# Stick-breaking attention with the queries on the partitions: a reversed scan of sigmoids, turned by TensorE, times differences of the values

## The reference

```python
def stick_breaking_attention(q, k, v):
    # beta[t,s] = sigmoid(q_t.k_s / sqrt(Dh)), s < t
    # A[t,s]    = beta[t,s] * prod_{s<j<t} (1 - beta[t,j])
    ...
        z = jnp.einsum("bqhd,bkhd->bhqk", qb, kb) * scale
        mask = s_idx < t_idx
        log_beta = jax.nn.log_sigmoid(z)
        log_one_minus = jnp.where(mask, jax.nn.log_sigmoid(-z), 0.0)
        tail = lax.cumsum(log_one_minus, axis=3, reverse=True) - log_one_minus
        weights = jnp.where(mask, jnp.exp(log_beta + tail), 0.0)
        outs.append(jnp.einsum("bhqk,bkhd->bqhd", weights, vb))

def second_block(...):
    h = rms_norm(x, norm1_g[layer])
    q, k, v, glu_a, glu_b = jnp.split(h @ w_in[layer], splits, axis=-1)
    q, k = rms_norm(q, q_norm_g), rms_norm(k, k_norm_g)      # per head
    attn = stick_breaking_attention(q, k, v)
    c = glu_a * jax.nn.sigmoid(glu_b)
    c = causal_depthwise_conv(c, conv_dw_w, conv_dw_b)
    c = jax.nn.silu(layer_norm(c, conv_ln_g, conv_ln_b))
    x = x + jnp.concatenate([attn, c], axis=-1) @ w_out
    ...
```

## Time and profile before

| | |
|---|---|
| median of 3 runs | 1230.31 us (1230.0 to 1230.79) |
| the profiled execution | 1230.45 us, its span 1228.7 us |
| TensorE busy | 1222.5 us, 99% of the span |
| weight loads of TensorE | 1004.1 us, beside the matmuls |
| VectorE, ScalarE, GpSimd busy | 593.9, 505.4, 585.3 us |
| granted clock of TensorE | full in all 40 slices |
| chain that ended last | TensorE 93%, VectorE 5%, ScalarE 1% |

### The profile page before, as it was taken

How to read it: one execution, slowest core, us unless ns; L and a number is a source line. 1 busy time by engine, 2 the same in 40 slices (tenths; PEclk the granted TensorE clock), 3 DMA queues, 4 the chain that set the end, 5 groups by cost and what they waited for, 6 DMA issues and landing times.

```text
span 1228.7 us, 16447 instructions
## 1 busy us (share of the span) xinstructions
PE 1222.5 (99%) x5590; PEld 1004.1 (82%) x5590; DVE 593.9 (48%) x870; ACT 505.4 (41%) x677; POOL 585.3 (48%) x473
## 2 busy tenths in 40 slices
PE   9999999999999999999999999999999999999998
PEld 7988888888888888888888886768888888888887
DVE  6782435434653165414675898764333223321431
ACT  7532443343443144323464247675433223332331
POOL 5875553233445344463465652134444434444444
PEclk9999999999999999999999999999999999999999
DMA  7444332122232322232233221102222322223222
GB/s 299 138 138 135 105 103 69 52 69 69 103 102 103 103 85 87 101 120 72 77 125 103 103 86 52 35 18 86 87 102 88 117 86 102 93 83 116 81 77 82
DMA packets 34035, 118.41 MB, mean 96 GB/s; under 512 B 4033, under 2 KB 4161, under 8 KB 33857
## 3 DMA queue, kind: packets, MB, share of 16 engines
q1 hardware_dynamic: 33696, 117.49, 27.9%
q10 hardware_dynamic: 288, 0.24, 0.1%
HBM read 115.61 MB, written 2.10 MB: 96 GB/s over the span
## 4 chain that ended last, share of the span: by engine, by line
PE 93%; DVE 5%; ACT 1%; POOL 0%; issue 0%; POOLq 0%
PE ps L1258 29%; PE ps L1259 29%; PE ps L1260 29%; DVE ps L1126 2%; DVE slab L1126 2%; PE ps L1582 2%; PE ps L1425 1%; PE ps L1563 1%; PE ps L1324 0%; PE ps L1350 0%; PE ps L1623 0%; POOL squares L443 0%; PE ps L1440 0%; PE ps L1399 0%; PE ps L1536 0%
## 5 line engine op out<-in xcount | busy, mean ns | idle before, releaser
L365 POOL TENSOR_TENSOR w_lo<-w_raw,w_hi 128x512 fp32r<-128x512 f32 x430 | 557.3, 1320 | 610.3 <-ACT w_hi L476 355.8
L1258 PE MATMUL ps<-xg_hi,w_hi 128*128 128x512 f32 x960 | 375.8, 391 | 0.0
L1260 PE MATMUL ps<-xg_hi,w_lo 128*128 128x512 f32 x960 | 373.6, 389 | 0.0
L1259 PE MATMUL ps<-xg_lo,w_hi 128*128 128x512 f32 x960 | 373.6, 389 | 0.0
L1258 PE MATMUL ps<-y_hi,w_hi 128*128 128x512 f32 (+1 forms) x608 | 230.9, 380 | 0.0
L1259 PE MATMUL ps<-y_lo,w_hi 128*128 128x512 f32 (+1 forms) x608 | 229.8, 378 | 0.0
L1260 PE MATMUL ps<-y_hi,w_lo 128*128 128x512 f32 (+1 forms) x608 | 229.8, 378 | 0.0
L1260 PEld LDWEIGHTS ps<-xg_hi,w_lo 128*128 128x128 f32 x960 | 180.2, 188 | 37.7
L1258 PEld LDWEIGHTS ps<-xg_hi,w_hi 128*128 128x128 f32 x960 | 180.2, 188 | 37.7 <-issue 0.8
L1259 PEld LDWEIGHTS ps<-xg_lo,w_hi 128*128 128x128 f32 x960 | 180.2, 188 | 37.3 <-issue 0.5
L476 ACT ACTIVATE w_hi<-w_raw 128x1024 fp32r<-128x1024 f32 x124 | 130.4, 1051 | 126.1 <-PE ps L1260 126.1
(11 more groups left out here) (218 smaller groups left out, 1064.1 us busy)
## 6 DMA issues: line engine op xcount, KB each, us to landing
w_raw<-weights SPq DMA_DIRECT2D x199, 512.0 KB, 3.2
w_raw<-weights SPq DMA_DIRECT2D x16, 384.0 KB, 2.9
out_t<-h SPq DMA_DIRECT2D x8, 256.0 KB, 2.0
h<-x_t SPq DMA_DIRECT2D x3, 512.0 KB, 8.3
slab<-mem_t SPq DMA_DIRECT2D x2, 512.0 KB, 10.6
slab<-mats_in SPq DMA_DIRECT2D x1, 1024.0 KB, 5.5
w_raw<-weights SPq DMA_DIRECT2D x2, 256.0 KB, 3.5
h<-x_t SPq DMA_DIRECT2D x2, 256.0 KB, 4.3
```

Source lines behind the costliest of these rows:

```text
L365: nc.gpsimd.tensor_tensor(w_lo[:, s, half], w_raw[:, s, half], w_hi[:, s, half].bitcast(F32), ALU.subtract).then_inc(done, 1)
L1258: pe.matmul(out, w[0], x[0], start=first, stop=False)
L1259: pe.matmul(out, w[0], x[1], start=False, stop=False)
L1260: return pe.matmul(out, w[1], x[0], start=False, stop=last)
```

## The change

The queries go on the partitions and the keys on the columns. A query tile t sees 128 (t+1) keys, so a head still fills 1280 columns. ScalarE writes the sigmoid of the scores, beta, to `took` and the sigmoid of their negative, 1 - beta, to the stick buffer. VectorE scans each of the four query tiles from the last key to the first: S[s] = (1 - beta[s]) S[s+1] + beta[s], in place in `took`, whose memory is that of the tiles 4 to 7 of `y_hi` and `y_lo`. The weight of a key is S[s] - S[s+1], and so the sum of weights times values equals the sum of S[s] (v[s] - v[s-1]). TensorE turns S tile by tile (`s_turn`, ten transposes of 128 x 128 to a head), ScalarE copies the 1280 columns out of PSUM, and `pair_values` multiplies by `v2`, which now holds the differences of the values.

For the differences ScalarE's queue issues two transfers after the scaling of `v2`: rows 0 to 126 of `v2` go to rows 1 to 127 of `v2_before`, and row 127 of the tiles 0 to 2 goes to row 0 of the tiles 1 to 3. GpSimd waits for both and subtracts in four instructions. `v2_before` shares memory with the stick buffer of head 1, so the sigmoids of head 1 wait for all four differences. Sigmoid and Ln/Exp need different function tables, and ScalarE loads one eight times more. The orders of the steps on TensorE, ScalarE, VectorE and GpSimd are written anew. The last tap group comes after the scan of head 7, and `ln_channel_sums(0)` after the output parts of blocks 1 and 2.

```diff
+        with nc.sbuf_tensor("took", [P, 2, DT * SEQ], F32) as took:
+            pass
...
+        v2_before = slab[:, 20 * SEQ + STICK:24 * SEQ + STICK].rearrange("p (m d) -> p m d", d=SEQ)
...
+        def took_of(hd):
+
+            return took[:, hd % 2, 4 * SEQ:4 * SEQ + STICK]
+
+        def backwards(ap):
+
+            return bass.AP(ap.tensor, ap.offset + ap.shape[1] - 1, [ap.ap[0], (-1, ap.shape[1])])
 
         def z_of(hd):
 
             return ps[:, 3 * (hd % 2):3 * (hd % 2) + 3, :].rearrange("p a t -> p (a t)")[:, 0:STICK]
 
-        QK_BANK = (4, 5, 6, 7, 6, 6, 7, 7)
...
+        QK_BANK = (4, 5, 6, 7, 6, 6, 7, 6)
...
+            nc.gpsimd.memset(v2_before[0:1, 0, :], 0.0).then_inc(v2_first, 1)
...
-            for b in range(QK, WOUT2):
+            weights_lo_next(QK)
+            pool.wait_ge(v2_shifted, 32)
+            for t in range(ST):
+                nc.gpsimd.tensor_tensor(v2[:, t, :], v2[:, t, :], v2_before[:, t, :], ALU.subtract).then_inc(v2_steps, 1)
+                if t % 2:
+                    weights_lo_next(QK + 1 + t // 2)
+            for b in range(QK + 3, WOUT2):
                 if b == QK + 4:
-                    pool.wait_ge(s_later, 2)
+                    pool.wait_ge(s_summed, 2 * ST)
...
+            act.wait_ge(v2_ready, ST)
+            act.wait_ge(v2_first, 1)
+            act.dma_start(v2_before[1:P, :, :], v2[0:P - 1, :, :]).then_inc(v2_shifted, 16)
+            act.dma_start(v2_before[0:1, 1:ST, :], v2[P - 1:P, 0:ST - 1, :]).then_inc(v2_shifted, 16)
             nc.scalar.preload_act_table_set("natural_log_exp_and_others")
 
-            def s_logs(hd):
-
-                t = stick_of(hd)
+            def s_parts_of(hd):
+
                 act.wait_ge(s_z, hd + 1)
+                if hd >= 2:
+                    act.wait_ge(s_turned, hd - 1)
+                if hd == 1:
+                    act.wait_ge(v2_steps, ST)
                 if hd >= 4:
                     act.wait_ge(s_out, (hd - 4) // 2 + 1)
-                for n, c in enumerate(log_parts(hd), log_parts_ahead(hd)):
-                    if hd == LAST_HEAD:
-                        act.wait_ge(s_last_min, 1)
-                        nc.scalar.activation(t[:, c], t[:, c], ACT.Exp).then_inc(s_exp, 1)
-                    else:
-                        nc.scalar.activation(t[:, c], z_of(hd)[:, c], ACT.Relu, scale=-1.0, bias=z_max[:]).then_inc(s_min, 1)
-                        act.wait_ge(s_min, n + 1)
-                        nc.scalar.activation(t[:, c], t[:, c], ACT.Exp, scale=-1.0, bias=z_max[:]).then_inc(s_exp, 1)
-                    act.wait_ge(s_exp, n + 1)
-                    nc.scalar.activation(t[:, c], t[:, c], ACT.Ln, bias=1.0).then_inc(s_log, 1)
+                nc.scalar.activation(took_of(hd), z_of(hd), ACT.Sigmoid).then_inc(s_parts, 1)
+                nc.scalar.activation(stick_of(hd), z_of(hd), ACT.Sigmoid, scale=-1.0).then_inc(s_parts, 1)
+
+            def table(name):
+                nc.scalar.preload_act_table_set(name)
...
-                for part, c in enumerate((FIRST, REST)):
-                    act.wait_ge(s_cum, 2 * hd + (2 if hd == SPLIT_HEAD else part + 1))
-                    nc.scalar.activation(stick_of(hd)[:, c], z_of(hd)[:, c], ACT.Exp).then_inc(s_att, 1)
+                act.wait_ge(s_turned, hd + 1)
+                nc.scalar.activation(stick_of(hd), z_of(hd), ACT.Copy).then_inc(s_att, 1)
...
-            s_logs(0)
+            table(SIGMOIDS)
+            s_parts_of(0)
             qk_squares_of(3)
-            s_logs(1)
+            s_parts_of(1)
+            table(LOGS)
             qk_squares_of(4)
             qk_rstd_of(3)
             s_weights(0)
             s_weights(1)
             qk_rstd_of(4)
 
-            s_logs(2)
-            pair_values_hi(0)
-            s_logs(3)
+            table(SIGMOIDS)
+            s_parts_of(2)
+            s_parts_of(3)
+            table(LOGS)
             qk_squares_of(5)
-            qk_squares_of(6)
             qk_rstd_of(5)
             s_weights(2)
             s_weights(3)
...
-            def s_softplus(hd):
-
-                t = stick_of(hd)
-                later = later_sums[:, hd % 2, :]
-                for n, c in enumerate(log_parts(hd), log_parts_ahead(hd)):
-                    dve.wait_ge(s_log, n + 1)
-                    if c == FIRST:
-                        nc.vector.tensor_tensor(t[:, c], z_of(hd)[:, c], t[:, c], ALU.max).then_inc(s_stick_first, 1)
-                        continue
-                    nc.vector.tensor_tensor(t[:, c], z_of(hd)[:, c], t[:, c], ALU.max).then_inc(s_stick, 1)
-                    dve.wait_ge(s_stick, hd + 1)
-                    if hd >= 2:
-                        dve.wait_ge(s_cum, 2 * (hd - 1))
-                    for dst, x, y in ((later[:, 0:P], t[:, AT[2] + P:AT[2] + 2 * P], t[:, AT[3]:AT[3] + P]),
-                                      (later[:, P:2 * P], t[:, AT[1] + P:AT[1] + 2 * P], t[:, AT[2]:AT[2] + P])):
-                        nc.vector.tensor_tensor(dst, x, y, ALU.add).then_inc(vstep, 1)
-                        own.tick()
-                    dve.wait_ge(vstep, own.now())
-                    nc.vector.tensor_tensor(later[:, 2 * P:3 * P], t[:, AT[1] + 2 * P:AT[1] + 3 * P], later[:, 0:P],
-                                            ALU.add).then_inc(s_later, 1)
+            def s_scan(hd):
+
+                dve.wait_ge(s_parts, 2 * hd + 2)
+                for bank, at, n in TILES:
+                    c = slice(bank * SEQ + at, bank * SEQ + at + n)
+                    took = backwards(took_of(hd)[:, c])
+                    nc.vector.tensor_tensor_scan(took, backwards(stick_of(hd)[:, c]), took, 0.0, ALU.mult,
+                                                 ALU.add).then_inc(s_summed, 1)
 
...
-            conv_taps(7)
-
-            s_softplus(0)
+            conv_taps(6)
+
+            s_scan(0)
+            s_scan(1)
             qk_input(4)
-            s_softplus(1)
+            conv_taps(2)
             qk_apply(3)
+            conv_taps(3)
+            qk_apply(4)
+            conv_taps(6)
+
+            s_scan(2)
...
-            dve.wait_ge(s_z, LAST_HEAD + 1)
-            dve.wait_ge(s_out, (LAST_HEAD - 4) // 2 + 1)
-            nc.vector.tensor_scalar(stick_of(LAST_HEAD), z_of(LAST_HEAD), Z_MAX, None, ALU.min).then_inc(s_last_min, 1)
-            s_softplus(6)
+            conv_taps(3)
+
+            s_scan(6)
             pair_values_lo(2)
-            s_softplus(7)
-            ln_centre()
+            s_scan(7)
+            conv_taps(len(tap_order))
             assert not tap_order
             pair_values_lo(3)
+            ln_centre()
...
-                elif t == 6:
-                    pe.wait_ge(y_lo_ready, Y_MIX2 + 1)
+                elif t >= 6:
+                    pe.wait_ge(y_lo_ready, Y_MIX2 + t - 5)
                 else:
-                    pe.wait_ge(qk_ready, {4: 3, 5: 5, 7: 7}[t])
+                    pe.wait_ge(qk_ready, {4: 3, 5: 5}[t])
...
-                for tile in (0, 1, 3, 2):
-                    bank, at, n = TILES[tile]
-                    if j >= 1 and tile < 2:
-                        pe.wait_ge(s_att, 2 * (2 * j - 1) + tile + 1)
+                if j >= 1:
+                    pe.wait_ge(s_att, 2 * j)
+                for t in (3, 2, 0, 1):
+                    bank, at, n = TILES[ST - 1 - t]
                     for hd in heads:
                         r = slice(HD * (hd % 2), HD * (hd % 2) + HD)
-                        pe.matmul(ps[:, 3 * (hd % 2) + bank, at:at + n], k2[r, j, tile * P:(tile + 1) * P],
-                                  q2[r, j, tile * P:], start=tile != 3, stop=False, skip_group_check=True)
+                        pe.matmul(ps[:, 3 * (hd % 2) + bank, at:at + n], q2[r, j, t * P:(t + 1) * P],
+                                  k2[r, j, 0:n], start=t != 0, stop=False, skip_group_check=True)
...
-            def s_cumulate(hd):
...
+            def s_turn(hd):
+
+                for n, t in enumerate((3, 2, 1, 0)):
+                    bank, at, _ = TILES[ST - 1 - t]
+                    pe.wait_ge(s_summed, ST * hd + n + 1)
+                    for key in range(t + 1):
+                        src = bank * SEQ + at + key * P
+                        to = AT[key] + (t - key) * P
+                        mm = pe.transpose(z_of(hd)[:, to:to + P], took_of(hd)[:, src:src + P], ident[:])
+                mm.then_inc(s_turned, 1)
...
+                if j == 0:
+                    pe.wait_ge(v2_steps, ST)
...
-                        if tile < 2:
-                            pe.wait_ge(s_att, 2 * hd + tile + 1)
+                        pe.wait_ge(s_att, hd + 1)
...
-            s_cumulate(0)
-            s_cumulate(1)
+            s_turn(0)
+            s_turn(1)
             qk_sum(4)
 
             pair_scores(1)
+            qk_block(5)
             pair_values(0)
-            qk_block(5)
+            qk_sum(5)
+            s_turn(2)
+            s_turn(3)
+
+            pair_scores(2)
```

(30 more changed lines are left out.)

118 lines of the change are left out of this document (40 added, 78 removed).

## The result

| | before | the change |
|---|---|---|
| median | 1230.41 us (1230.0 to 1230.79, 4 runs) | 1271.28 us (1270.16 to 1271.94, 4 runs) |
| profiled execution, its span | 1230.45, 1228.7 us | 1271.29, 1269.6 us |
| TensorE busy from 718 us to the first residual of WOUT2 | 116.23 us | 112.29 us |
| TensorE idle there | 1.11 us | 45.82 us |

The change is slower: ratio 1.0331, 95% interval 1.0313 to 1.0349. The forecast was 1267 in a range of 1237 to 1282. The time is near, but two of the terms behind it were off in opposite directions, as the experiments show.

What follows compares the result with a forecast made beforehand. It took TensorE as the bound, busy 1222.5 of 1228.7 us. Work shed -19.1, waits +21.8, scans and shared path +4.5, transfer +29.7 sum to +36.9 on 1230.45, median 0.14 below: 1267 us, range 1237 to 1282.

Steps and rivals of the forecast that it cites:

- The transfer: Shift of value rows before GpSimd's subtractions: one DMA engine moves all 127 rows, landing at 769.3; +29.7 us.
- One wait of nearly 30 us: Sign in the trace: TensorE waits once, nearly 30 us, at the turn of head 1.
- Pair 1: TensorE waits 1.2 us for product and square after turning head 1, then 3.7 before the scores for both copies.
- Pair 2: Before this pair's scores, TensorE waits 1.8 us for sum, factor and two copies.
- Pair 3: TensorE waits 0.5 us for the late last square, then 3.3 before the scores.
- Tile 2: Output part of this tile: TensorE waits 2.5 us for `y_lo(2)`, behind four sigmoids, a table load and the split.
- Copy 7: ScalarE's copy before the last values: TensorE waits 1.1 us.
- Tail: Layer norm's chain, now late in TensorE's list: waits of 3.7, 3.05 and 2.1 us, together 8.85.
- Scans: VectorE's scans, three quarters from tap to GpSimd's pass, with VectorE and GpSimd hindering each other: +4.5 us, ends 0 and 11.
- What TensorE sheds: Cumulation of eight heads (27.8 us) gives way to ten transposes a head (8.7): -19.1 us.
- The table loads: Eight more on ScalarE, 1.28 us each without added drain; ScalarE's total hardly moves, loads on the path counted in the waits.
- The rival of a spread transfer: Transfer lands in some 6 to 8 us and the 29.7 fall away: 1238 us, from 1233 to 1244; chance 0.22.

Runs made afterwards that it cites:

- e1_even: The change with its 127-row transfer issued as two, of 112 and 15 rows: 1248.27 us, ratio to before 1.0139.
- e10_halves: The change with its 127-row transfer split in two by the second dimension, each still of 127 rows: 1277.97 us.
- e2_small_first: The change with its two transfers issued in the other order, the small one first: 1271.11 us.
- e4_no_shift: The change without both transfers; GpSimd subtracts another tile instead, so the values' differences are not those of the computation: 1247.41 us.
- e8_short_scans: e1_even with each of the 32 scans over 128 columns instead of 128 to 512, other sums left out: 1240.86 us.
- e5_keep: e1_even with useless matmuls in five of TensorE's waits, same computed result: 1243.38 us, ratio 1.0110.

## Why the prediction was right, and where not

- **The transfer** is the term that decided, and it held: one engine, landing forecast at 769.3, seen at 765.1. The page "DMA: Bandwidth & Descriptors" of the Trainium skill ("Why a DMA increments its semaphore by 16 and not by 1") has one engine for 127 partitions, and the runs agree with it: 6.5 us for 112 rows in e1_even, 46 for 127, a DMA share of one in sixteen while they move, and in e10_halves a second transfer of 127 rows brings no gain. Its price was put too high: 29.7 us forecast, 23.0 measured by e1_even. The turn of head 1 was expected at 750.9 without the transfer; in e1_even it starts at 756.7, behind waits of 1.76 before the scores of pair 0, 1.20 before block 4 and 0.56 before the first turn, which the working had passed over. From there to the change's 778.7 it is 22.0.
- **One wait of nearly 30 us** before the turn of head 1 was wrong for the change: it shows 15.93 us at the first sum and 7.91 at the turn. "GpSimd's first subtraction idle until then, ScalarE idle before head 1's sigmoid" came true, but the prediction cost an issue at nothing, and the second issue held ScalarE for 19.14. e2_small_first shows that this cost 1.5 us at the turn and nothing in the total.
- **The waits of pairs and tail.** Pair 1: forecast 1.2 and 3.7, seen 0.60 and 2.40. Pair 2: 1.8, seen 1.59 in e1_even. Pair 3: 0.5 and 3.3, seen 0.35 and 2.89. Tile 2: 2.5, seen 1.56. Copy 7: 1.1, seen 0.3. Tail: 8.85, seen 7.53. Each stands where the working put it and is somewhat shorter. Slow matmuls hide some of it: pair 1's 2.40 stands behind a sum that takes 2.08 us at half clock, and in e4_no_shift, where that sum takes 1.12, the wait is 3.35. Missed was 1.97 before block 7.
- **Scans**: 2.97 us a head, where three quarters of the way between tap and GpSimd's pass gave 2.9. The Trainium skill (DVE: opcode table, instruction layouts, handler registers and perf-mode slots, "Datapath and trigger behaviour") says half throughput: 2.32 ns a column here against a tap's 1.3, so the trace nearly agrees. e8_short_scans puts all of the term, with the clock that follows, at 7.4 us or more; 4.5 was low, and 0 to 11 held it.
- **What TensorE sheds** failed as a size: 19.1 forecast, some 14.5 near full clock (e5_keep), 3.9 in the change. The transposes are busy for 1.57 us a head (12.6 for eight in e5_keep) where 1.09 was forecast. A row of ten takes 1.25 to its end, and where a wait follows the end counts too; heads 0, 1 and 7 are turned in pieces as the strips come, 0.66 for four and 1.23 for six, each with its own run-out. With short scans (e8_short_scans) all eight take 9.86.
- **The clock** had no term, as the prediction said of itself. It is some 10.6 us in the change (14.5 less 3.9). The windows show 0.50 in and behind each long wait, and lower clocks behind short waits too. The prediction looked for it behind the one long wait alone. The Trainium skill (TensorE: Matmul & The Clock Gate, "Part 1: The HAM clock gate") says that it halves when TensorE idles, and the windows around the two long waits agree.
- **The table loads**: the load at 739.51 takes 1.28 us, and the next instruction starts 1.30 after its start; there is no drain behind it, as the prediction read from the earlier trace rows.
- **So the sum came near by luck, because errors cancelled**: waits 11.3 below the forecast (44.7 for 56.0), work 15.2 above it (-3.9 for -19.1). 36.9 - 11.3 + 15.2 is 40.8. The rival of a spread transfer shows the same error without cover: 1238 forecast, 1248.3 measured, outside its 1233 to 1244.

## What to carry to other kernels

Count a transfer's rows by how they can be dealt out: 112 and 15 rows landed in 6.5 and 7.5 us, 127 took 46, and an issue behind such a long one-engine transfer held the engine that issued it for 19 us. When an edit takes work off a TensorE that never waited and puts short waits in its place, much of the shed time is not saved: here the granted clock fell with such waits, and the remaining matmuls paid some 10 to 11 us. Price the clock before moving lists about; here filler in the waits gave 4.9 us, and two reorderings 0 and 1.
